# One transformer layer on one core: modulation rows by DMA, and whole expert weights per transfer

## The reference, cut to what matters

```python
m = silu(cond) @ mod_w + mod_b               # 6 rows of D: shift1, scale1, gate1, shift2, scale2, gate2
h = rmsnorm(x) * (1 + scale1) + shift1
...                                          # attention and convolution branches, gated -> mix input
mix = (g_attn * attn_out + g_conv * conv_out) @ w_out
x = x + gate1 * mix
h2 = rmsnorm(x) * (1 + scale2) + shift2
# 64 experts, 8 chosen for a token, and one shared expert
hid = silu(h2 @ exp_w_gate[e]) * (h2 @ exp_w_up[e]) * gates[:, e]     # 1024 -> 256, twice
x = x + gate2 * (sum_e(hid @ exp_w_down[e]) + shared(h2))             # 256 -> 1024
y = rmsnorm(x) * final_g
```

## Time and profile before

| | us |
|---|---|
| median of 3 runs | 1304.66 (1301.41 to 1308.7) |
| the profiled execution | 1304.72 |
| its span, first to last instruction | 1302.6 |
| PE busy | 1151.5 (88%) |
| DVE busy | 1067.8 (82%) |
| ACT busy | 797.4 (61%) |

### The profile page before, as it was taken

How to read it: one execution, slowest core, us unless ns; L and a number is a source line. 1 busy time by engine, 2 the same in 40 slices (tenths; PEclk the granted TensorE clock), 3 DMA queues, 4 the chain that set the end, 5 groups by cost and what they waited for, 6 DMA issues and landing times.

```text
span 1302.6 us, 17353 instructions
## 1 busy us (share of the span) xinstructions
PE 1151.5 (88%) x5707; PEld 945.0 (73%) x5707; DVE 1067.8 (82%) x1456; ACT 797.4 (61%) x1018; POOL 215.9 (17%) x144
## 2 busy tenths in 40 slices
PE   3899999789989999698999999999999999999800
PEld 1599999654558967677887877788888888887600
DVE  2769999999976734566988889899999899998648
ACT  5553333567766422336877777788878778887601
POOL 1000000300000000011521212224435123142100
PEclk9799999889999979589999999999999999999955
DMA  8563456325436153428999999999999999999396
GB/s 313 170 167 97 138 161 176 117 65 162 162 117 206 65 176 119 165 93 293 376 355 343 365 340 361 345 354 357 360 341 370 348 350 368 357 357 338 140 341 244
DMA packets 142044, 328.05 MB, mean 252 GB/s; under 512 B 28053, under 2 KB 69352, under 8 KB 133159
## 3 DMA queue, kind: packets, MB, share of 16 engines
q1 hardware_dynamic: 120424, 294.66, 64.3%
q0 software_dynamic: 19264, 29.57, 6.2%
q10 hardware_dynamic: 2304, 3.15, 0.7%
HBM read 325.06 MB, written 44.19 MB: 283 GB/s over the span
## 4 chain that ended last, share of the span: by engine, by line
PE 31%; DMA 28%; DVE 26%; issue 6%; ACT 6%; SPq 2%; DVEq 0%; POOL 0%; ACTq 0%; POOLq 0%
DMA raw<-in_exp_w_down_dram 23%; PE bank L1548 9%; PE bank L1550 9%; PE bank L1549 9%; DVE lo L1434 7%; DVE lo L1439 5%; ACT hi L950 4%; DVE lo L1038 3%; DVE zb L1139 2%; DMA raw<-in_mod_w_dram 2%; SPq L595 2%; DMA slots<-sh_d 1%; DVE slots L1502 1%; DVE mx L1214 1%; DMA y_d<-ys,ixt 1%
## 5 line engine op out<-in xcount | busy, mean ns | idle before, releaser
L1434 DVE TENSOR_TENSOR lo<-raw,hi 128x2048 fp32r<-128x2048 f32 x128 | 292.5, 2286 | 5.9 <-ACT hi L943 5.9
L943 ACT ACTIVATE hi<-raw 128x2048 fp32r<-128x2048 f32 x128 | 244.2, 1909 | 4.9 <-issue 4.9
L1548 PE MATMUL bank<-hi,xgh 128*128 128x512 f32 x512 | 209.6, 409 | 10.6 <-DVE lo L1434 9.9
L1550 PE MATMUL bank<-hi,xgl 128*128 128x512 f32 x512 | 201.1, 393 | 0.0
L1549 PE MATMUL bank<-lo,xgh 128*128 128x512 f32 x512 | 199.8, 390 | 0.0
L950 ACT ACTIVATE hi<-raw 128x2048 fp32r<-128x2048 f32 x64 | 122.8, 1919 | 115.4 <-DMA raw<-in_exp_w_down_dram 115.4
L1439 DVE TENSOR_TENSOR lo<-raw,hi 128x2048 fp32r<-128x2048 f32 x64 | 146.7, 2293 | 51.0 <-ACT hi L950 50.7
L1038 DVE TENSOR_TENSOR lo<-raw,hi 128x2048 fp32r<-128x2048 f32 (+2 forms) x65 | 142.3, 2195 | 47.8 <-ACT hi L726 47.8
L726 ACT ACTIVATE hi<-raw 128x2048 fp32r<-128x2048 f32 (+2 forms) x65 | 119.0, 1834 | 33.2 <-PE bank L1550 28.0
L694 POOL DMA_INDIRECT y_d<-ys,ixt x64 | 129.3, 2021 | 50.2 <-ACT ys L981 30.5
L1139 DVE SCALAR_TENSOR_TENSOR zb<-zb,cwt 128x400 f32<-128x400 f32 x240 | 135.5, 636 | 0.6
(11 more groups left out here) (286 smaller groups left out, 2161.0 us busy)
## 6 DMA issues: line engine op xcount, KB each, us to landing
raw<-in_exp_w_gate_dram SPq DMA_DIRECT2D x128, 512.0 KB, 6.5
raw<-in_exp_w_up_dram SPq DMA_DIRECT2D x128, 512.0 KB, 10.8
raw<-in_exp_w_down_dram SPq DMA_DIRECT2D x64, 1024.0 KB, 12.2
raw<-in_mod_w_dram SPq DMA_DIRECT2D x24, 1024.0 KB, 5.3
slots<-y_d SPq DMA_DIRECT2D x6, 2048.0 KB, 15.4
raw<-in_w_in_dram SPq DMA_DIRECT2D x16, 512.0 KB, 5.4
raw<-in_w_in_dram SPq DMA_DIRECT2D x8, 1024.0 KB, 5.3
raw<-in_w_o_attn_dram SPq DMA_DIRECT2D x4, 1024.0 KB, 4.9
```

The costliest lines, as they stand in the source:

```text
L943: act.activation(dst, src, ACT.Copy).then_inc(ghi_done, 1)
L1434: dve.tensor_tensor(l, src, h.bitcast(F32), ALU.subtract).then_inc(glo_done, 1)
L1548: pe.matmul(out, ah, bh, start=first, stop=False)
L1550: return pe.matmul(out, al, bh, start=False, stop=last)
```

## The change

Rows of the modulation: `modr2` has four rows. POOL copies the bias row into each of two rows of a DRAM tensor `mod_d` and then adds the two parts of each condition group to them by accumulating DMAs, in two rounds with a wait between. gate1, scale2 and shift2 are read back by DMAs that repeat one row of 4 KB for 128 partitions (`partition_broadcast`), issued from POOL behind waits for `m_done` and for the last `pw2` result; DVE makes `a2` in place in `scales2`, between b = 0 and b = 1. gate2 is read straight from `mod_d` in the tail, and `g2`, `g2_d` and the spill are gone, as are `rows_of` on PE and ACT and 16 bank groups.

Expert weights: gate goes to the first gate/up buffer whole, up to the second, in one transfer of 1 MB with 8 KB a partition each. ACT and DVE write their 128 x 2048 results into two tiles `hgu` and `lgu` in which gate and up alternate by 256; they lie where `hi` and `lo` of both halves lay. PE waits once, for both. The diff leaves out the declarations of semaphores and of `g2`.

```diff
--- before.py
+++ after.py
@@ -120,9 +120,7 @@
     g += [("mean",), ("wo", 0), ("wo", 1), ("var",)]
     g += [("wo", j) for j in range(2, KD)]
     g += [("pw2", j) for j in range(KD)]
-    g += [("bc", v, c, b) for v in (2, 4, 3) for c in range(2) for b in range(2)]
     g += [("wout", b, t) for b in range(2) for t in range(NT)]
-    g += [("bc", 5, c, b) for c in range(2) for b in range(2)]
     g += [("h2T", c) for c in range(KD)]
     g += [("rt", t) for t in range(NT)]
     for t in range(NT):
@@ -183,7 +181,7 @@
         kr = sb("kr", [P, 4 * RD], A + 7.375)
         x = sb("x", [P, NT, D], A + 8)
-        modr2 = sb("modr2", [5, 8 * 512], A + 8)
+        modr2 = sb("modr2", [4, 8 * 512], A + 8)
         zb = sb("zb", [P, KD + 2, ZW], A + 24)
         zh = sb("zh", [P, KD + 2, ZW], A + 24, F32R)
         hTh = sb("hTh", [P, KD, T], A + 41, F32R)
@@ -229,7 +227,6 @@
         g2row = sb("g2row", [P, D], A + 120)
         a2 = sb("a2", [P, 2, D], A + 25)
         b2 = sb("b2", [P, 2, D], A + 33)
-        g2 = sb("g2", [P, 2, D], A + 41)
         h2p = sb("h2p", [P, NT, D], A + 53)
         junk2 = sb("junk2", [P, D], A + 113)
         h2h = sb("h2h", [P, KD, T], A + 81, F32R)
@@ -261,6 +258,9 @@
         raw += [sb(f"raw{i}", [P, IW], A + 25 + 8 * (i - 4)) for i in (4, 5)]
         hi += [sb(f"hi{i}", [P, IW], A + 41 + 8 * (i - 3), F32R) for i in (3, 4, 5)]
         lo += [sb(f"lo{i}", [P, IW], A + 65 + 8 * (i - 3), F32R) for i in (3, 4, 5)]
+        gu_at = (32, A + 41), (56, A + 65)
+        hgu, lgu = ([sb(f"{n}{i}", [P, KD, 2, FF], at, F32R) for i, at in enumerate(ats)]
+                    for n, ats in zip(("hgu", "lgu"), gu_at))
         xg = [sb(f"xg{i}", [P, D], A + 89 + 4 * i) for i in range(2)]
         xgh = [sb(f"xgh{i}", [P, KD, P], A + 109 + 8 * i, F32R) for i in range(2)]
         xgl = [sb(f"xgl{i}", [P, KD, P], A + 113 + 8 * i, F32R) for i in range(2)]
@@ -284,7 +284,7 @@
         sig_d = dram("sig_d", [16, P, T])
         h2_d = dram("h2_d", [T, D])
         x1_d = dram("x1_d", [P, NT, D])
-        g2_d = dram("g2_d", [P, 2, D])
+        mod_d = dram("mod_d", [2, 4 * D])
         y_d = dram("y_d", [T * TOPK, D])
         sh_d = dram("sh_d", [P, NT, D])
...
...
...
@@ -481,6 +479,10 @@
         def hl(n):
             i = (item_no[n] - NI) % NHL
             return cut(hi[i], n), cut(lo[i], n)
+        def mod_row(v, cc):
+            return mod_d[1 - cc, D * (v - 2):D * (v - 1)].rearrange("(a n) -> a n", a=1)
         def cond_of(t):
             return 0 if t == 0 else 1
@@ -585,14 +587,12 @@
             def load_gate_up(i, k):
                 j = i * UNROLL + k
                 one = expert_of(j)
-                for q in range(2):
-                    s = 3 * (k % 2) + q
+                for w, src in enumerate((exp_w_gate, exp_w_up)):
+                    s = 3 * (k % 2) + w
                     if from_step(j, 2):
-                        sp.wait_ge(glo_done, 2 * (j - 2) + (q + 1))
-                    v = raw[s][:, :].rearrange("p (w n) -> p w n", w=2)
-                    for w, src in enumerate((exp_w_gate, exp_w_up)):
-                        sv = src[0, one].rearrange("a (p k) n -> (a p) (k n)", k=KD)
-                        sp.dma_start(v[:, w, :], sv[:, 1024 * q:1024 * q + 1024]).then_inc(xraw_in[s], 16)
+                        sp.wait_ge(glo_done, 2 * (j - 2) + (w + 1))
+                    sv = src[0, one].rearrange("a (p k) n -> (a p) (k n)", k=KD)
+                    sp.dma_start(raw[s][:, :], sv).then_inc(xraw_in[s], 16)
             def load_down(i, k):
                 j, s = i * UNROLL + k, 3 * (k % 2) + 2
@@ -638,7 +638,8 @@
                              rows[t * P:(t + 1) * P, :, 512 * b:512 * b + 512]).then_inc(slots_in[n % 4], 16)
                 sp.dma_start(slots[n % 4][:, TOPK, :], sh_d[:, t, 512 * b:512 * b + 512]).then_inc(slots_in[n % 4], 16)
                 if n == 0:
-                    sp.dma_start(tg[:, :, :], g2_d).then_inc(tail_in, 16)
+                    for cc in range(2):
+                        sp.dma_start(tg[:, cc, :], mod_row(5, cc).partition_broadcast(P)).then_inc(tail_in, 16)
                     sp.dma_start(fgr[:, :], final_g.rearrange("(a n) -> a n", a=1).partition_broadcast(P)).then_inc(tail_in, 16)
                 if b == 0:
                     if t >= 2:
@@ -664,16 +665,29 @@
             pool.wait_ge(krT_done, 1)
             pool.tensor_copy(kT[ND:HD, 1:H, :], kT[ND:HD, 0:1, :].to_broadcast([RD, H - 1, 512])).then_inc(krep_done, 1)
-            pool.wait_ge(xn_done, NT)
-            pool.dma_start(modr2[4:5, :], mod_b[:, 2048:6144]).then_inc(biasrow2_in, 16)
+            for cc in range(2):
+                pool.dma_start(mod_d[cc:cc + 1, :], mod_b[:, 2048:6144]).then_inc(mod_rows_out, 16)
+            pool.wait_ge(mod_rows_out, 32)
+            pool.wait_ge(mod_done, 12)
+            for part in range(2):
+                for cc in range(2):
+                    pool.dma_start(mod_d[cc:cc + 1, :], modr2[2 * cc + part:2 * cc + part + 1, :], accum_op=ALU.add,
+                                   max_dma_last_dim=4096).then_inc(mod_rows_out, 16)
+                pool.wait_ge(mod_rows_out, 64 + 32 * part)
+            pool.wait_ge(m_done, 2 * KD)
+            for cc in range(2):
+                pool.dma_start(g1[:, cc, :], mod_row(2, cc).partition_broadcast(P)).then_inc(g1_in, 16)
+            got(pool, ("pw2", 7))
+            for cc in range(2):
+                pool.dma_start(a2[:, cc, :], mod_row(4, cc).partition_broadcast(P)).then_inc(a2_in, 16)
+            for cc in range(2):
+                pool.dma_start(b2[:, cc, :], mod_row(3, cc).partition_broadcast(P)).then_inc(b2_in, 16)
             pool.wait_ge(x1_done, 2 * NT)
             pool.dma_start(x1_d, x1[:, :, :]).then_inc(x1_out, 16)
             for t in range(NT):
                 pool.wait_ge(h2_done, t + 1)
                 pool.dma_start(h2_d[t * P:(t + 1) * P, :], h2p[:, t, :]).then_inc(h2d_out, 16)
-            pool.wait_ge(bc_a, 12)
-            pool.dma_start(g2_d, g2[:, :, :]).then_inc(spill_out, 16)
             def gather(i, k):
                 j = i * UNROLL + k
@@ -901,15 +915,6 @@
                     act.wait_ge(m_done, KD + k + 1)
                     act.activation(mh[:, k, :], m[:, k, :], ACT.Copy).then_inc(mh_done, 1)
-            def rows_of(v, dst):
-                for cc in range(2):
-                    for b in range(2):
-                        p = got(act, ("bc", v, cc, b))
-                        act.activation(dst[:, cc, 512 * b:512 * b + 512], p[:, :], ACT.Copy).then_inc(bc_a, 1)
-            rows_of(2, g1)
-            rows_of(3, b2)
             for b in range(2):
                 split(item_no[("wout", b, 0)] + 2)
                 split(item_no[("wout", b, 1)] + 2)
@@ -920,7 +925,6 @@
                 act.activation(junk2[:, :], x1[:, t, :], ACT.Square, accum_out=stat[:, 40 + t:41 + t]).then_inc(ssq2_done, 1)
                 act.wait_ge(r2v, t + 1)
                 act.activation(stat[:, 48 + t:49 + t], stat[:, 44 + t:45 + t], ACT.Sqrt).then_inc(r2a, 1)
-            rows_of(5, g2)
             for k in range(KD):
                 p = got(act, ("h2T", k))
                 act.activation(h2h[:, k, :], p[:, 0:T], ACT.Copy).then_inc(h2h_done, 1)
@@ -933,14 +937,13 @@
             for t in range(NT):
                 p = got(act, ("shgu", t))
                 act.activation(shs[:, t, :], p[:, 0:FF], ACT.Silu).then_inc(shs_done, 1)
-            def gate_up_hi(i, k, q):
-                j, s = i * UNROLL + k, 3 * (k % 2) + q
-                act.wait_ge(xraw_in[s], uses(i, k) * 32)
+            def gate_up_hi(i, k, w):
+                j, s = i * UNROLL + k, 3 * (k % 2) + w
+                act.wait_ge(xraw_in[s], uses(i, k) * 16)
                 if from_step(j, 2):
                     act.wait_ge(gu_filled, j - 1)
-                src = raw[s][:, :].rearrange("p (w k n) -> p k w n", w=2, k=4)
-                dst = hi[s][:, :].rearrange("p (k w n) -> p k w n", w=2, k=4)
-                act.activation(dst, src, ACT.Copy).then_inc(ghi_done, 1)
+                src = raw[s][:, :].rearrange("p (k n) -> p k n", k=KD)
+                act.activation(hgu[k % 2][:, :, w, :], src, ACT.Copy).then_inc(ghi_done, 1)
             def down_hi(i, k):
                 j, s = i * UNROLL + k, 3 * (k % 2) + 2
@@ -1009,7 +1012,6 @@
                     p = got(act, ("shd", t, b))
                     act.activation(shy[:, t, 512 * b:512 * b + 512], p[:, :], ACT.Copy).then_inc(shy_done, 1)
             turn_hi(0, 0)
-            act.wait_ge(spill_out, 16)
             act.wait_ge(sh_out, 16)
             in_order(act, step)
@@ -1277,14 +1279,15 @@
                     dve.wait_ge(mh_done, k + 1)
                     dve.tensor_tensor(ml[:, k, :], m[:, k, :], mh[:, k, :].bitcast(F32), ALU.subtract).then_inc(ml_done, 1)
-            dve.wait_ge(g2row_in, 16)
-            for cc in range(2):
-                for b in range(2):
-                    g = ("bc", 4, cc, b)
```

(58 more changed lines are left out.)

8 lines of the change are left out of this document (3 added, 5 removed).

## The result

The changed kernel takes 1296.43 us (median of 16 runs, 1291.3 to 1301.23), the one before 1304.74 (16 runs, 1301.41 to 1311.13): 8.3 us less, a ratio of 0.9926 with a 95% interval of 0.9911 to 0.9941. The forecast was 1285.2, a gain of 19.5 us: the direction and the range held, the size did not.

The account below looks back on a forecast made before the run. The prediction took the loop to stand on PE, with late down weights pushing through DVE. Front -9.5, loop -10.4 and tail +0.4 sum to -19.5 us, from 1304.7 to 1285.2 us, range 1276 to 1299.5.

Parts of the forecast that it names:

- Waits of 0.78 on down weights should fall by at least the 0.67: Expert loop: 8 KB rows save 0.67 us of DMA time an expert, so DVE's waits shrink and PE sets the pace.
- Of 0.78 us, 0.54 are DVE's slack and 0.24 reach PE: Expert loop before: of DVE's average wait per expert for down weights, its slack hides 0.54 and PE loses 0.24.
- The new wait: Loop: PE waits for both splits before starting an expert; paid once at the loop's start, +2.65 us.
- The front: Ahead of the loop: removing row matmuls saves up to 16.2 us on PE, crowded w_out loads leave -9.5 us.
- If the clock stays up: Front: w_out matmuls of b = 0 take 0.23 us each, running from 467.7 to 484.2.
- in its order: Front: DVE works through its own list after w_out lands, ending with the shared expert's split at 503.5 us.
- Hidden things: POOL's DRAM additions, with 90 us of cover, and gate2's row work in PE's gap count nothing; the tail adds 0.4 us.
- Bytes bind: First rival: bytes, not rows, limit the loop, which then loses 2.6 us; 1298.2 us in all, chance 0.17.
- PE idles in each expert: Slower rival: DVE never catches up and each expert pays at PE's new wait; 1323 us at 10.4 an expert, chance 0.05.
- free front: Rival: the front gains its full 15.4 us, the loop 13.4; 1276.3 us in all, chance 0.15.
- choked front: Rival: broadcasts and weights together move only 250 GB/s, so the front gains 2 us; 1292.7 us in all, chance 0.12.
- The rule against the change: Loop: a limit of about 358 GB/s per core makes row size worth nothing, so the loop comes out at +2.6 us.

Follow-up runs that it names:

- e1: Only the row part of the change: the changed kernel with the expert weights loaded, split and waited for as in the kernel before; 1295.88 us.
- e3: The changed kernel with the down weights issued between gate and up instead of behind both; 1281.54 us.
- e10: The kernel before, with its down transfer issued between the two halves of gate/up and 4 KB rows kept; 1288.81 us.
- e14: The changed kernel with each gate and up weight in two half-row transfers and down issued between gate and up; 1291.41 us.
- e15: The changed kernel loading only the first half of each row of the down weights from expert 2 on; 1281.57 us.
- e5: The kernel before, with PE waiting for both splits of an expert ahead of its first gate/up matmul; 1306.22 us.
- e4: The changed kernel with both w_out transfers of b = 1 issued ahead of the reload of x and g2row and the broadcasts; 1286.19 us.
- e7: The changed kernel with the broadcasts of scale2 and shift2 held until ACT has copied the last w_out; 1292.01 us.
- e12: The changed kernel with each gate and up weight in two transfers of 64 partitions each, 8 KB rows kept; 1771.01 us.
- e16: The kernel before, with a step's two transfers reading both halves of one weight's rows instead of one half of gate and of up; 1336.82 us.
- e13: The changed kernel with each 1 MB gate or up transfer described in 4 KB pieces; 1311.34 us.
- e11: The changed kernel with each 1 MB gate or up transfer described in 1 KB pieces; 1322.80 us.

## Why the prediction was right and wrong

- **What bounds the loop: right, but half seen.** "PE, with late down weights pushing through DVE" is what the waits show. The prediction didn't ask what made them late.
- **The step that failed:** "Waits of 0.78 on down weights should fall by at least the 0.67". It took DMA time saved for waiting time saved, and the busy share for the time that the rows need. The saving itself came (0.45 us an expert, DMA share 0.97 to 0.92), but down stood behind a wait and a transfer of `up` that the change left in place. It landed after 12.3 us instead of 12.0, DVE's waits for it fell from 46.0 to 40.0 us only, and PE stayed at 9.86. From expert 3 on -13.05 was forecast (with 3 us of stalls left) and -4.95 measured, of which e1 shows some 2 without the change; 13.0 us of stalls were left (591.30 against e3's 578.28). e3, e10, e14 and e15 show that the ring through down was the cause: opened, or with a shorter landing, it lets PE run at its floor.
- **An average where the stalls come in stretches.** "Of 0.78 us, 0.54 are DVE's slack and 0.24 reach PE" spreads the waits evenly over the experts. They don't lie so: PE ran at 9.67 in 900 to 1000 us and stalled in 700 to 800. The waits of PE before were also 18.0 us and not 16.05, as the floor for these 60 experts is 578.28 us (e3) and not 580.2.
- **The new wait: right.** +2.65 forecast at the start, +2.3 measured; not paid in each expert (e5, e15).
- **The front: the price right in kind, the last step wrong, the gain too large.** -9.5 forecast, -6.7 in this profile, -5.3 as a mean over profiles. `w_out` came at 487.1 instead of 485.3. "If the clock stays up" didn't hold: the granted clock was 0.59 in 468 to 472 behind a pause of 2.39 us, and 0.50 in 490 to 494 behind the pause of 5.93 before b = 1, with matmuls at 0.43. The forecast let x1 follow "in its order" from DVE's own list, at 503.5; it came at 506.36. DVE was on that list up to the router split, done at 501.05 where 501.3 was forecast (the two scale operations took 2.35 us together instead of 4.1), and then idle for 3.10 us: the next split needs ACT's copy, and that waited for PE until 502.20. The prediction names this wait for the kernel before and leaves it out here. e4 and e7 show that the crowd ahead of `w_out` was the price. (The 13.8 us by which `wout` could start sooner are 13.9 by the rows: 465.29 + 16.24 - 467.62.)
- **Hidden things: right.** POOL's additions in DRAM went out at 377 and 381 us, 85 us ahead of use; the tail cost 0.5 instead of 0.4.
- **The sum.** -9.5 - 10.4 + 0.4 was forecast, -6.7 - 2.7 + 0.5 measured in the profiles. The range held only because it had room for the first rival.
- **The rivals.** "Bytes bind" gave 1298.2, near the measured time, but for the wrong reason: its loop was to lose 2.6, it gained 2.7, and the front gave less. And bytes don't bind: e3 moves the same bytes with no stall, 375 GB/s in 700 to 800 us, where the changed kernel stalled at 356. "PE idles in each expert", "free front" and "choked front" didn't come.
- **The rule against the change.** The Trainium skill's limit of about 358 GB/s (DMA: Bandwidth & Descriptors, section Where 436 GB/s comes from) isn't what stopped it: here one core runs, and 384 GB/s flowed in 476 to 480, 375 over 100 us of e3. The trace doesn't agree with it as a limit. At the floor the loop needed 356 (e3, 900 to 1000).

Left open: why the landing differs by stretches (13.4 us in 700 to 800, 11.1 in 900 to 1000); why two transfers of the halves of the same rows, or 4 KB pieces, land the next one later while the DMA engines have idle time; and what holds a down transfer for 12 us when it is issued behind `up`, and 7.7 when ahead of it.

## What to carry to other kernels

A stall on a late transfer isn't cured by making transfers cheaper. Look first at what the issuing engine waits for ahead of it, and close the ring: landing, copy, subtraction, buffer free, issue. If that ring, divided by the buffers in it, is near the pace, move the issue; here one line's place gave 15 us, where the cheaper rows gave 2 from expert 3 on. Don't read a busy share near 1 as the bound: e3 has 0.98 and no stall. And hold windows against the stretches in which the stalls lie. When work is taken out ahead of a product, check which weights it wants next, and load those before what the same step also sends.

## What the runs showed of the hardware

- Transfers onto 64 partitions: 196 GB/s with the DMA engines at 0.98 (e12), against 354 onto 128 (the changed kernel); they slow the whole loop, to 17.8 us an expert.
- The same transfers in another order: DMA engines busy 0.98 instead of 0.92 at 356 and 354 GB/s, and 1 MB landing after 7.7 us instead of 12.3 (e3 and the changed kernel).
- The same 0.5 MB transfers cost 31 us more when two in a row read the two halves of the same rows instead of rows of two weights (e16).
- One 1 MB transfer with its 8 KB rows cut to 4 KB or 1 KB pieces costs the kernel 15 or 26 us (e13, e11).
- The granted clock was 0.59 in 468 to 472, after PE had been idle for 2.39 us, and 0.50 in 490 to 494, after 5.93 us idle (the changed kernel). Before, it was 0.50 in 476 to 480 in the row matmuls, with PE busy throughout.
